# Two-layer encoder trunk on 8 cores: four weight tiles of the first mixer in the FFN's slots, and another transfer rate in the planner

## The reference

```
h = RMSNorm(x);  z = h @ W_in                    # 1024 -> 2048 columns
x += W_out @ concat[ sliding-window attention, gated conv of width 3,
                     chunked gMLP gating, multi-scale pooling ]
x += W_down @ (silu(g) * val),  [g, val] = causal_dwconv3(W_up @ RMSNorm(x))
```

## Time and profile before

| | |
|---|---|
| runs, median (lowest to highest) | 3413.86 us (3225.46 to 3414.59) |
| the profiled execution | 3223.0 us |
| its span, slowest of the 8 cores | 3221.5 us (the others 3204.2 to 3220.0) |
| PE busy (matmuls) | 2894.4 us, 90% of the span |
| DVE, ACT, POOL busy | 64%, 54%, 41% |
| DMA moved | 474.00 MB, mean 147 GB/s |

### The profile page before, as it was taken

The page is one execution under the profiler, slowest core; times in us unless marked ns, Lnnn a source line. Parts: engine busy times, 40 slices in busy tenths (PEclk is TensorE's granted clock), DMA queues, the critical chain, the costliest instruction groups (busy, mean ns, idle before and its releaser), DMA issues.

```text
span 3221.5 us, 57637 instructions; the slowest of 8 cores (3204.2 to 3221.5 us)
## 1 busy us (share of the span) xinstructions
PE 2894.4 (90%) x15818; PEld 1365.9 (42%) x15818; DVE 2046.2 (64%) x4480; ACT 1730.0 (54%) x3486; POOL 1316.1 (41%) x1481
## 2 busy tenths in 40 slices
PE   4488789978899999999999999999999999999997
PEld 2244344434444444444444444444444444444443
DVE  3356656666476575857577585757667585757663
ACT  2256446465365655637475554737465564747463
POOL 0136435255154352616244241625345261626342
PEclk7689899989999999999999999999999999999999
DMA  7357675676754544444454534444454544434343
GB/s 180 89 123 170 142 196 148 153 170 172 180 171 133 181 134 135 138 134 150 121 190 128 182 126 132 143 137 138 125 180 139 169 130 138 147 121 150 120 151 118
DMA packets 157023, 474.00 MB, mean 147 GB/s; under 512 B 17880, under 2 KB 20390, under 8 KB 156582
## 3 DMA queue, kind: packets, MB, share of 16 engines
q1 hardware_dynamic: 141990, 422.74, 40.9%
q0 software_dynamic: 14720, 47.59, 9.3%
HBM read 452.71 MB, written 65.12 MB: 161 GB/s over the span
## 4 chain that ended last, share of the span: by engine, by line
PE 63%; DVE 14%; issue 9%; ACT 6%; DMA 4%; POOL 3%; DVEq 0%; SPq 0%; ACTq 0%; POOLq 0%
PE psb L593 62%; DVE cc L581 4%; ACT cc L570 2%; ACT L570 1%; DVE Pn L985 1%; POOL cc L584 1%; DVE hnM L581 1%; DVE scr L581 1%; DVE gv L832 1%; POOL act L584 1%; PE psb L706 1%; DVE ast L969 1%; ACT ct L570 1%; DMA y_p<-scr 1%; DMA io<-st_m 1%
## 5 line engine op out<-in xcount | busy, mean ns | idle before, releaser
L593 PE MATMUL psb<-hnF,wsF 128*128 128x512 bf16 x5632 | 1299.1, 383 | 62.1 <-DVE fhalo L587 18.6
L581 DVE SCALAR_TENSOR_TENSOR cc<-psb,coltS,cc 128x510 f32<-128x510 f32 (+3 forms) x1188 | 804.1, 690 | 325.4 <-ACT ct L570 154.4
L593 PEld LDWEIGHTS psb<-hnF,wsF 128*128 128x128 bf16 x5632 | 545.8, 99 | 727.5 <-issue 128.6
L593 PE MATMUL psb<-act,wsF 128*128 128x512 bf16 x2816 | 664.7, 388 | 11.2 <-DVE fhalo L587 2.7
L570 ACT ACTIVATE cc<-psb,coltS 128x512 f32<-128x512 f32 (+1 forms) x792 | 498.6, 641 | 324.0 <-PE psb L593 317.7
L584 POOL TENSOR_TENSOR cc<-cc,ct 128x511 f32<-128x511 f32 (+1 forms) x396 | 472.5, 1193 | 320.5 <-DVE fhalo L587 201.7
L584 POOL TENSOR_TENSOR act<-cc 128x512 bf16<-128x512 f32 x352 | 462.3, 1318 | 146.1 <-ACT cc L570 89.6
L593 PE MATMUL psb<-hnM,wsM 128*128 128x512 bf16 x1664 | 401.6, 387 | 42.8 <-DVE hnM L581 20.0
L578 DVE TENSOR_TENSOR xT<-psb,xT 128x512 f32<-128x512 f32 (+1 forms) x288 | 180.1, 633 | 393.2 <-PE psb L593 393.0
L593 PEld LDWEIGHTS psb<-act,wsF 128*128 128x128 bf16 x2816 | 268.3, 99 | 338.7 <-issue 56.7
L584 POOL TENSOR_TENSOR cc<-cc,hcon 128x4 f32<-128x4 f32 x264 | 63.5, 241 | 835.8 <-DVE fhalo L587 793.6
(11 more groups left out here) (159 smaller groups left out, 2478.7 us busy)
## 6 DMA issues: line engine op xcount, KB each, us to landing
wsF<-im_u SPq DMA_DIRECT2D x308, 512.0 KB, 3.7
wsM<-im_m SPq DMA_DIRECT2D x168, 512.0 KB, 3.7
wsF<-im_d SPq DMA_DIRECT2D x224, 352.0 KB, 3.0
wsF<-wu POOLq DMA_DIRECT2D x44, 512.0 KB, 7.7
im_u<-wsF SPq DMA_DIRECT2D x44, 512.0 KB, 7.4
y_p<-scr SPq DMA_DIRECT2D x64, 256.0 KB, 3.7
io<-x_p SPq DMA_DIRECT2D x56, 256.0 KB, 4.6
wsM<-wm POOLq DMA_DIRECT2D x24, 512.0 KB, 7.7
```

The lines of the kernel that those rows point to most:

```text
L581: V(lambda e: e.scalar_tensor_tensor(out=out, in0=in0, scalar=scalar, in1=in1, op0=op0, op1=op1), reads, writes, n, "stt", psum)
L593: ins = e.matmul(o, lhsT=l_, rhs=r_, start=st, stop=sp_)
```

## The change

Two things. In `wload`, the first time through the mixer's tiles, tiles 3 to 6 take the slots `wsF0` to `wsF3` instead of going round the `wsM` ring, and their loads are held back by the gate. m7 then takes the slot of m0, m8 that of m1, m9 that of m2, m10 that of m7, m11 that of m8, and the next mixer's first tile that of m9. The ring of the FFN does not move: u0 takes `wsF0` and now waits for the last matmul on m3 and for its store, u1 for m4, u2 for m5, u3 for m6. The other is the constant `DMA_BW` of the planner, 290e3 bytes per microsecond instead of 230e3, from which the whole order of instructions is worked out anew.

```diff
-    DMA_BW = 230e3
+    DMA_BW = 290e3
...
             def wload(kind, idx):
                 n = HK * 128 if kind == "d" else 2048
-                if kind == "m":
+                fs = idx - NWM if kind == "m" and not cnt.get("started") else -1
+                if 0 <= fs < NWF:
+                    t, key, semk = wsF[fs], ("wsF", fs), f"dwf{fs}"
+                    src, img = wm_d, im_m
+                    if fs == NWF - 1:
+                        cnt["started"] = 1
+                elif kind == "m":
                     si = ring("wsM", NWM)
...
-                    S.dma("pool", lambda e: e.dma_start(out=t[:, 0:n], in_=src[idx]), semk, writes=[key], nbytes=n * 128 * 4, after=gate if kind != "m" else ())
+                    S.dma("pool", lambda e: e.dma_start(out=t[:, 0:n], in_=src[idx]), semk, writes=[key], nbytes=n * 128 * 4, after=gate if kind != "m" or fs >= 0 else ())
```

## The result

The changed kernel takes 3123.01 us in the median of 4 runs (3121.14 to 3123.97). Against the kernel before the ratio is 0.9685, 95% interval 0.9662 to 0.9708: 3.15% faster, 100 us. In some executions of several kernels the cores of one die run at a lower granted clock and the time is several per cent longer (the four runs of before have a median of 3319.66 us), so the times and ratios in this text are of the other executions alone, which for before lie at 3223.3 and 3225.5 us.

The account below looks back on a forecast made before the run. Matmuls were taken to bound the kernel (PE busy 90%), with gains where PE idles: 3223.0 us less 46.5 for the opening's loads and 16 for the planner's rate gave 3161 us, range 3125 to 3205.

Parts of the forecast that it names:

- The loads of m3 to m6: Opening: m3 to m6 land early in FFN slots, so PE's waits for mixer tiles go; 46.5 us gained.
- The 12.1 us that I took off for DVE: Opening: DVE is the longer engine by 12.1 us in the windows pushed together, taken off the gain in full.
- the 58.6: Opening: three stretches that lose their cause, 24.4, 21.4 and 12.8 us, together 58.6 us before the deduction for DVE.
- My 24.5 us of PE work: Opening, from 64.3 us to the conv's end: PE has gv and conv, 24.5 us, against DVE's 36.6.
- My reading of the cause: Opening: three slots for twelve tiles is what it waits for, with two loads, 8.57 and 11.01 us, on the chain.
- The loads of u0 to u3: Opening: issued later, they have over 60 us to land against 20.9 needed; cost nothing.
- The rival that the start gives back: Opening gains only 26 us, as shared engines and u loads take some back, and the order nothing; about 3197, chance 0.22.
- The planner's rate: All instructions, mainly steps 1 and 3: the order planned at 290 cuts PE's idle time; 16 us gained.
- 30% of the excess idle time: Steps 1 and 3: share taken of 53 us excess idle PE, since the mixer's parts keep their ACT and DVE chains; 16 us.
- the bound of 53 us: Steps 1 and 3: upper bound on the rate's gain, their excess idle PE over steps 2 and 4.
- The order pays in full: Rival: steps 1 and 3 come near 210 us, opening gains 46 and order 45; 3132 us, chance 0.18.
- The slower rival: Steps 1 and 3: the order counts on tiles too early and PE waits, 1.5 us late each giving 3291; chance 0.06.

Follow-up runs that it names:

- the slots alone: Changed kernel with DMA_BW back at 230, m3 to m6 still in FFN slots: 3172.8 us, ratio 0.9833 to the kernel before.
- rate_only: Kernel before with only DMA_BW raised from 230 to 290, three-slot ring kept: 3148.8 us, ratio 0.9757.
- Light_before: Kernel before, same order, each FFN conversion load reading a bf16 tile (half the bytes, no cast): 3214.0 us, ratio 0.9960.
- the four rates: Changed kernel with DMA_BW at 230, 260, 290 and 340: 3172.8, 3142.8, 3123.0 and 3145.8 us.
- light_after: Changed kernel, same order, each FFN conversion load reading a bf16 tile (half the bytes, no cast): 3114.7 us, ratio 0.9653.

## Why the prediction was right in direction and short in size

**The loads of m3 to m6, 46.5 us taken, 54.5 measured with both parts, 50.9 with the slots alone.** The mechanism held: gv at 65.6 us (said: near 65), conv at 73.7 (before 80), no wait for a mixer tile, `W_out` at 127.1 (131 to 140), first FFN matmul at 150.9 (near 160). The 12.1 us that I took off for DVE were too many: of the 58.6 only 4.1 stayed away with both parts, and 7.7 with the slots alone. My 24.5 us of PE work left out the attention's own matmuls, most of the 10.8 us in the window from 62 to 88, so DVE was ahead of PE by less than I said; attention did go under the pooling, and the dense stretch ran at full clock (1.00 from 62 to 88 us). My reading of the cause was half right: rate_only shows that the opening can lose 35 us with three slots as well, in another order.

**The loads of u0 to u3, nothing taken.** Right. They left at 74.9 and by 92 us, were never waited for, and no `W_out` tile was late. The rival that the start gives back has no support left. I had also said that the opening fills the DMA engines only in the wait for m7; the rows that I had begin at 62 us, and from 38 to 53 us the kernel before has a DMA share of 1.01.

**The planner's rate, 16 us taken: this is the step that failed.** The two steps gave 64.8 us, and after 4.3 lost in step 2 and 15.3 from step 4 on, 45.2 net. Four things were wrong in it. First, I took 30% of the excess idle time on the ground that the mixer's parts keep their own chains of ACT and DVE "whatever the rate"; but the row of the "u" loads, one each 7.0 us against 6.8 planned, already said that the chip walks at the pace of the list, and after the change it was 5.4 against 5.4. Light_before shows it from the other side. Second, the excess was mis-sized: my windows ended steps 1 and 3 at 437 and 870 us, 12 and 23 us early. Cut at their true ends, steps 1 to 4 hold 41.5, 11.7, 46.9 and 4.8 us of idle PE, so the excess is 72 us and not 53; of it 42 went. Third, I counted idle PE only. A step that idles less also ran at a higher clock, 0.92 to 0.98 in step 1, and that is 9 us there on top (in step 3 matmul time fell by 13.5, part of it the 40 matmuls that went to step 4); so the bound of 53 us was no bound. Fourth, I let the later steps move either way by 10 us; they moved one way, by 15, and the four rates say that this belongs to the rate.

**The rivals.** "The order pays in full" (3132, chance 0.18) was the nearest. It was still 9 us too slow, with 46 us for the opening where 54.5 came and 45 for the order where 45.2 came. The slower rival, tiles that the plan has landed and the chip has not, is real but small: at 290 light_after finds 6 to 10 us of it in the two steps by the medians (13 on the slowest cores). At 340, 23 us slower, PE waits for weights only 1 to 3 us longer than at 290, so late tiles do not explain that loss by PE's own waits.

## What to carry to other kernels

Where an order is written out ahead by a planner, compare the spacing of a repeated issue in the trace with what the planner's table gives for it: if they agree and the transfers could do better, the table sets the time. Here the two stretches in question gave 65 us, of which 45 were left after what other steps lost by the same constant. So set the rate for the stretch with most transfers, and look at the other stretches by themselves. Cut the stretches where they end and on all cores before you size what they hold. When a tile waits for a slot, ask who the last reader is and where it stands in the order, before giving the tile another slot.

## What the runs showed of the hardware

Less idle time on PE came with less matmul time, 9 us on 21 in step 1, at a granted clock of 0.98 instead of 0.92. Halving the bytes read and dropping the cast took POOL's queue from 44.8% to 24.6% of the engines' time for the same 16.78 MB written; the light load reads half the bytes and does not cast, and the runs do not tell the two apart. And in the crowd behind the gate the 256 KB load of the sample's state took over 20 us to land, from 30.5 to 52.2 us, beside 4 MB of weights, with the DMA engines full (a share of 1.02) from 38 to 53 us.

```profile
38.00:53.00 15.00, 2.36 (x13) 1.45 (x12) 4.13 (x7) 0.63 (x3) 0.00 (x0) 0.50 1.02 197
```
